# Expert stage: U rows gathered and dotted first, half of V's columns read densely and multiplied on TensorE

## The reference, cut to what matters

```python
q = (hblk @ w_q).reshape(b_, PEER_BLOCK, PEER_HEADS, 2, PEER_QDIM // 2)
s1 = einsum('bthd,hnd->bthn', q[..., 0, :], k1)   # 8 heads, 128 keys
s2 = einsum('bthd,hnd->bthn', q[..., 1, :], k2)
v1, i1 = top_k(s1, 16); v2, i2 = top_k(s2, 16)
cand = v1[..., :, None] + v2[..., None, :]        # 16 x 16 sums
score, pos = top_k(cand, 16)
idx = (i1 * 128 + i2 at pos)                      # one of 16384 experts
gate = softmax(score)
act = gelu(einsum('bthkd,btd->bthk', w_u[idx], hblk))
out = einsum('bthk,bthkd->btd', gate * act, w_v[idx])
```

## Time and profile before

| | |
|---|---|
| median of 3 runs | 2938.45 us (2937.06 to 2939.99) |
| profiled execution, span | 2939.0 us |
| PE busy | 2628.4 us (89%) |
| DVE busy | 1949.4 us (66%) |
| ACT busy | 979.2 us (33%) |
| POOL busy | 556.7 us (19%) |
| DMA | 901.77 MB, of that 604.02 MB by POOL's queue |
| granted PE clock | 0.988 of full speed |

### The profile page before, as it was taken

The page is one execution under the profiler, slowest core; times in us unless marked ns, Lnnn a source line. Parts: engine busy times, 40 slices in busy tenths (PEclk is TensorE's granted clock), DMA queues, the critical chain, the costliest instruction groups (busy, mean ns, idle before and its releaser), DMA issues.

```text
span 2939.0 us, 30782 instructions
## 1 busy us (share of the span) xinstructions
PE 2628.4 (89%) x11045; PEld 1777.7 (60%) x11045; DVE 1949.4 (66%) x2654; ACT 979.2 (33%) x1335; POOL 556.7 (19%) x580
## 2 busy tenths in 40 slices
PE   7999998999999999999999897777878877777777
PEld 3588886888777899998888753332434333232232
DVE  4679997444676788887555866666556656556646
ACT  5577776433564443334444211111101111111110
POOL 0000000000000000000000453433333333333333
PEclk9999999999999999999999999999999999999999
DMA  8733334542425888887566899999999999999998
GB/s 351 278 108 114 114 129 158 189 170 101 154 90 233 332 322 335 322 336 279 203 247 266 357 422 421 421 421 421 421 421 421 421 421 421 421 421 422 422 421 342
DMA packets 126356, 901.77 MB, mean 307 GB/s; under 512 B 14000, under 2 KB 15536, under 8 KB 17200
## 3 DMA queue, kind: packets, MB, share of 16 engines
q0 software_dynamic: 82944, 604.02, 49.8%
q1 hardware_dynamic: 38448, 276.84, 25.1%
q10 hardware_dynamic: 4864, 19.61, 1.7%
HBM read 898.29 MB, written 2.13 MB: 306 GB/s over the span
## 4 chain that ended last, share of the span: by engine, by line
PE 53%; DMA 35%; DVE 6%; issue 4%; ACT 1%; POOL 0%; POOLq 0%; SPq 0%; ACTq 0%; DVEq 0%
DMA u<-in_peer_u,idx 32%; PE ps L476 12%; PE ps L519 8%; PE ps L521 8%; PE ps L520 8%; PE ps L491 6%; DVE u L2042 3%; PE ps L882 2%; DMA v<-in_peer_v,idx 2%; PE ps L599 2%; PE ps L905 1%; DMA w<-in_stream 1%; PE ps L533 1%; PE ps L711 1%; PE ps L694 1%
## 5 line engine op out<-in xcount | busy, mean ns | idle before, releaser
L905 PE MATMUL ps<-v,dg 128*128 128x512 f32 x1920 | 894.4, 614 | 252.3 <-DMA v<-in_peer_v,idx 212.2
L2042 DVE SCALAR_TENSOR_TENSOR u<-u,hN 128x2048 f32<-128x2048 f32 x256 | 586.6, 2292 | 459.8 <-DMA u<-in_peer_u,idx 459.4
L905 PEld LDWEIGHTS ps<-v,dg 128*128 128x128 f32 x1920 | 356.4, 194 | 784.9 <-issue 427.9
L1383 DVE TENSOR_TENSOR wl<-w,wh 128x1024 fp32r<-128x1024 f32 x428 | 519.7, 1222 | 359.2 <-ACT wh L1018 358.8
L1018 ACT ACTIVATE wh<-w 128x1024 fp32r<-128x1024 f32 x428 | 451.3, 1059 | 607.9 <-PE ps L521 405.6
L2148 POOL DMA_INDIRECT u<-in_peer_u,idx x256 | 257.6, 1006 | 933.0 <-DVE u L2042 543.5
L476 PE MATMUL ps<-both,wh 128*128 128x256 f32 x2048 | 371.8, 284 | 0.0
L1326 ACT ACTIVATE dg<-con,wt 128x128 f32<-128x128 f32 x240 | 92.7, 399 | 807.4 <-PE ps L905 802.4
L476 PEld LDWEIGHTS ps<-both,wh 128*128 128x128 f32 x2048 | 320.1, 192 | 3.5 <-issue 3.3
L476 PE MATMUL ps<-both,wl 128*128 128x256 f32 x1024 | 289.8, 283 | 0.0
L2132 POOL DMA_DIRECT2D mr<-in_wmod x64 | 34.1, 534 | 1322.8 <-DVE br_lo L1791 912.7
(11 more groups left out here) (297 smaller groups left out, 2893.5 us busy)
## 6 DMA issues: line engine op xcount, KB each, us to landing
w<-in_stream SPq DMA_DIRECT2D x258, 1024.0 KB, 4.9
mr<-in_wmod POOLq DMA_DIRECT2D x64, 1024.0 KB, 6.9
wg<-in_gates ACTq DMA_DIRECT2D x8, 512.0 KB, 3.2
wx<-in_stream SPq DMA_DIRECT2D x4, 1024.0 KB, 7.9
u<-in_peer_u,idx POOLq DMA_INDIRECT x256
v<-in_peer_v,idx POOLq DMA_INDIRECT x256, 18.0
xs<-in_ctx ACTq DMA_DIRECT2D x1, 2048.0 KB, 7.6
xs<-in_x ACTq DMA_DIRECT2D x1, 2048.0 KB, 14.6
```

The lines of the kernel that those rows point to most:

```text
L905: last = mm(ps[:, b, :], dg[:, k % 4, :], V[n % NV][:, b * 512:(b + 1) * 512], start=(k == 0), stop=(k == TOPK - 1))
L1383: tt(wl[p % SPLITS][:, :, :], W[s][:, q * PIECE:(q + 1) * PIECE, :], wh[p % SPLITS][:, :, :].bitcast(F32), ALU.subtract)\
L2042: stt(U[n % NU][:, :], U[n % NU][:, :], 1.0, hN[t][:, :], ALU.mult, ALU.mult, accum_out=dot[:, t, k:k + 1])\
```

## The change

All 256 U rows are now gathered first, in the order `ORDER`: turn (0,0), turn (1,0), then heads 1 to 7 of tile 0, then heads 1 to 7 of tile 1. There are eight buffers `U`. All dots are on DVE (`ON_POOL` is empty); from the third turn on the tokens' tile is read from a copy in PSUM banks 0 to 3 that ACT makes (`spread_h`), except in turn 9.

When all rows of a tile are dotted, its 128 weights per token are worked out at once. V is then handled in two halves of 1024 columns:

- Columns 0 to 1023 are dense. For each token n a matrix of 128 x 128 weights over all experts is made: DVE writes two one-hot tiles over the token's 128 slots (`onehot`: `oa` for the first index, `ob` for the second index times the weight), PE multiplies them (`token`), and ACT copies four such matrices into `WT[t]` (`store_weights`). Tile 0's tokens are spread over the dots of tile 1 (`TOKEN_AT`, from row 149 to row 251); tile 1's come after all dots. Then PE runs over 128 blocks j of V, each a dense 0.52 MB load by SP into one of six buffers `VD`, four matmuls each (`dense`), into PSUM banks 0 to 3.
- Columns 1024 to 2047 are gathered, 256 half-rows of 4 KB per token into four buffers `VG`, and DVE adds each, times its weight, to `acc` (`gathered`).

Both halves of V are laid out as arrays of their own. The modulation row `m5r` is loaded by DMA instead of being spread by PE, and the last operations work on halves.

```diff
+DC = 1024
+ORDER = [(0, 0), (1, 0)] + [(0, h) for h in range(1, PH)] + [(1, h) for h in range(1, PH)]
+ON_POOL = ()
+ROUTE_AT = (1, 2, 4, 6, 7, 9, 11, 12, 14)
+TURN0 = 9
+TOKEN_AT = {n: TURN0 * TOPK + 5 + n * 103 // P for n in range(P)}
...
-        NU, NV = 4, 8
+        NU, NG, ND = 8, 4, 6
@@ @block.sync
+            for j in range(NKEYS):
+                if j == 0:
+                    sp.wait_ge(*AR.at(PH - 1, "q"))
+                elif j == 2:
+                    sp.wait_ge(*PR.at(2 * PH - 1, "s"))
+                elif j == 4:
+                    sp.wait_ge(*VG_.at(1, "g1"))
+                elif j >= ND:
+                    sp.wait_ge(dense_done, j - ND + 1)
+                sp.dma_start(VD[j % ND][:, :], a_vd[j]).then_inc(vd_in[j % ND], 16)
@@ @block.tensor
+            def token(t, n):
+                m = t * P + n
+                pe.wait_ge(onehots, m + 1)
+                if m % 4 == 0 and m >= 8:
+                    pe.wait_ge(w_stored, m // 4 - 1)
+                mm(ps[:, (4, 7)[m // 4 % 2], n % 4 * P:(n % 4 + 1) * P], oa[m % 6][:, :], ob[m % 6][:, :], start=(n % 4 == 0), stop=True,
+                   skip_group_check=True).then_inc(w_made, 1)
+            def dense(j):
+                pe.wait_ge(vd_in[j % ND], 16 * (j // ND + 1))
                 for t in (0, 1):
+                    for b in range(DB):
+                        last = mm(ps[:, DB * t + b, :], WT[t][:, j, :], VD[j % ND][:, b * 512:(b + 1) * 512], start=(j == 0), stop=(j == NKEYS - 1))
...
+            tables(1)
+            for n in range(P):
+                token(1, n)
+            pe.wait_ge(w_stored, 2 * P // 4)
+            for j in range(NKEYS):
+                dense(j)
@@ @block.scalar
+            def store_weights(g):
+                t, n = divmod(4 * g, P)
+                act.wait_ge(w_made, 4 * g + 4)
+                fn(WT[t][:, :, n:n + 4].rearrange("p i t -> p t i"), ps[:, (4, 7)[g % 2], :].rearrange("p (t i) -> p t i", t=4), ACT.Copy).then_inc(w_stored, 1)
@@ @block.vector
+            def onehot(t, n):
+                m = t * P + n
+                if m >= 6:
+                    dve.wait_ge(w_made, m - 5)
+                tsc(oa[m % 6][:, :], iota_k[:, :], i1T[:, n:n + 1], None, ALU.is_equal)
+                tsc(ob[m % 6][:, :], iota_k[:, :], i2T[:, n:n + 1], wT[:, n:n + 1], ALU.is_equal, ALU.mult).then_inc(onehots, 1)
+            def gathered(m):
+                t, c = m % 2, m // 2
+                dve.wait_ge(vg_in[m % NG], 16 * (m // NG + 1))
...
+                    dve.wait_ge(summed, m - 1)
+                    stt(acc[:, t, :], VG[m % NG][:, :], dot[:, t, c:c + 1], acc[:, t, :], ALU.mult, ALU.add).then_inc(summed, 1)
...
+            for r in range(ROWS):
+                q, k = divmod(r, TOPK)
+                t, h = ORDER[q]
...
+                    hv = hN[t][:, :] if q in (0, 1, TURN0) else ps[:, 0:4, :].rearrange("p b n -> p (b n)")
+                    dve.wait_ge(u_in[r % NU], 16 * (r // NU + 1))
+                    stt(U[r % NU][:, :], U[r % NU][:, :], 1.0, hv, ALU.mult, ALU.mult, accum_out=dot[:, t, h * TOPK + k:h * TOPK + k + 1])\
+                        .then_inc(dve_dots, 1)
+                if (q == 0 and k) or (q == 1 and k < 14) or (q > 1 and k in ROUTE_AT):
+                    next(routes, None)
...
+                for n in range(P):
+                    if TOKEN_AT[n] == r:
+                        onehot(0, n)
+            gelu_inner_of(1)
+            weights_of(1)
+            copy_tables(1)
+            for n in range(P):
+                onehot(1, n)
+                if n % 8 == 7:
+                    gathered(n // 8)
+            for m in range(P // 8, ROWS):
+                gathered(m)
@@ @block.gpsimd
+            for m in range(ROWS):
+                t, c = m % 2, m // 2
+                if m == 0:
+                    pool.wait_ge(*VR.at(2 * PH - 1, "idx"))
+                elif m == 1:
+                    pool.wait_ge(dve_dots, dots_by(ROWS - 1))
+                elif m == 3:
+                    pool.wait_ge(*VG_.at(1, "w"))
+                elif m >= NG:
+                    pool.wait_ge(summed, m - NG + 1)
```

More of the change, by code:

```diff
@@ L399, in build, with dots_by, pool_by, row_used @@
+        def dots_by(r):
+            return sum(1 for n in range(r + 1) if n not in ON_POOL)
+        def pool_by(r):
+            return sum(1 for n in ON_POOL if n <= r)
+        def row_used(r):
+            return (act_dots, pool_by(r)) if r in ON_POOL else (dve_dots, dots_by(r))
+        PRIMED_V = [VT, VL] + VO + [VS, VW]
+        PRIMED_A = [AD, AL] + AO + [AS]
+        PRIMED_P = [PL]
         block = ctx.enter_context(nc.Block())
@@ L896, in experts @@
[L896 to L920, removed]
+                pe.wait_ge(*VR.at(q - 2, "ib1"))
@@ L942, in _ @@
-            for h in range(PH):
-                if h == PH - 1:
-                    spread_m5()
-                experts(h, 0)
-                if 6 <= h + 4 < PH:
-                    route(h + 4)
-                if h + 1 < PH:
-                    experts(h, 1, h + 2 if h + 2 < PH else None)
-            last_half()
+            queries(1)
+            scores(2)
+            queries(2)
+            scores(3)
+            queries(3)
+            queries(4)
+            scores(4)
+            queries(5)
@@ new lines, in _ @@
+            queries(6)
+            scores(5)
+            queries(7)
+            for q in range(6, TURN0 + 4):
+                scores(q)
+            pe.wait_ge(*AR.at(PH - 1, "q"))
+            tables(0)
+            for q in range(TURN0, 2 * PH):
+                for n in range(P):
+                    if TOKEN_AT[n] // TOPK == q:
+                        token(0, n)
+                if q + 4 < 2 * PH:
+                    scores(q + 4)
+            tables(1)
+            for n in range(P):
+                token(1, n)
@@ new lines, in _ @@
+            assert next(routes, None) is None
+            gelu_inner_of(1)
+            weights_of(1)
+            copy_tables(1)
+            for n in range(P):
+                onehot(1, n)
[3 more added lines that the diff above has]
+                gathered(m)
+            dve.wait_ge(m5_in, 16)
+            dve.wait_ge(summed, ROWS)
+            for t in (0, 1):
+                tt(acc[:, t, :], acc[:, t, :], m5r[:, DC:D], ALU.mult).then_inc(*VX.inc(f"m{t}"))
+                dve.wait_ge(*VX.at(0, f"m{t}"))
+                tt(x2[:, t, DC:D], x2[:, t, DC:D], acc[:, t, :], ALU.add).then_inc(*VX.inc(f"o{t}"))
@@ L2132, in _, with product @@
                 pool.dma_start(mr[n % NM][:, :], a_wmod[n]).then_inc(mr_in[n % NM], 16)
[L2134 to L2136 removed]
+            def product(r):
+                t, _ = ORDER[r // TOPK]
+                pool.wait_ge(u_in[r % NU], 16 * (r // NU + 1))
+                nc.gpsimd.tensor_tensor(U[r % NU][:, :], U[r % NU][:, :], hN[t][:, :], ALU.mult).then_inc(pool_products, 1)
+            for r in range(ROWS):
+                q, k = divmod(r, TOPK)
+                if r == 0:
```

566 lines of the change are left out of this document (257 added, 309 removed).

## The result

The changed kernel takes 3056.45 us (median of 4 runs, 3046.63 to 3060.48) against 2938.48 us: a ratio of 1.0399, 95% interval 1.0381 to 1.0416. It is slower, as forecast, but by 118 us and not by 47. The profiled execution is the shortest of the four runs, with a span of 3044.8 us.

A forecast was written before the change was run, and what follows sets the result against it. DMA bytes were taken to bound the expert stage. From 1631.9 us, stage A was to end at 2417, B at 2505, C at 2971, and a 14 us tail gave 2985, 1.6% slower; range 2925 to 3055.

The forecast's parts named there:

- stage A: All 256 U dots, routing and tile 0's one-hots: bound by DVE at 780 us plus 5 for hiccups, ending at 2417.
- stage B: Weights and one-hots of tile 1 after all dots, DMA nearly idle: 88 us, ending at 2505.
- stage C: Dense product beside the gathered half of V, gathers ending last: 466 us, to 2971.
- tail: Last sum, last operations on halves and the store: 14 us, to 2985.
- PE in stage C: The dense product's matmuls, 3.43 us for each of 128 blocks: 439 us.
- The gathers in stage C: Half-rows of V at 2.0 us each beside the dense product, 219 in 439 us, then 17 at 1.6.
- The turn of a buffer: One gather buffer's gap, issue, landing, sum and 0.6 for POOL held up: 6.3 us for four buffers, 1.6 a gather.
- PE last: Rival for the stage's end: gathers keep up at 1.96 us, dense product runs without wait; end 2951, chance 0.16.
- Dearer one-hots or 4 KB descriptors: Rival: one-hot pairs at 0.64 us (+36) or descriptors at 393 GB/s (+30); end 3015 to 3050, chance 0.18.
- Nearly free one-hots: Rival in stage A and stage B: 0.30 us a pair, 51 us less; end 2900, half effect 2925; chance 0.16.
- POOL starved: Rival in stage C: every gather issue waits under a DVE sum, 2.4 us a gather; end 3085, chance 0.08.
- signs named for a wrong forecast: Stage A ending before 2380 or after 2450, trough under 60 us, PE dense waits over 20, POOL issues above 1.8.

The follow-up runs named there:

- the kernel with six blocks: The changed kernel with 122 of the 128 dense blocks of V left out, loads and matmuls; span 2968.9 us.

## Why the prediction was wrong

The direction, the three stages and the engine that ends last were right; the size of one term was not. Term by term, with the forecast against the profiled span, which is 10 us under the median span (against the median time the forecast is off by 71):

| step | forecast | measured | difference |
|---|---|---|---|
| first dot | 1631.9 | 1626.8 | -5 |
| stage A | 785 | 772 | -13 |
| stage B | 88 | 80 | -8 |
| stage C | 466 | 552 | +86 |
| tail | 14 | 13 | -1 |
| end | 2985 | 3044.8 | +60 |

- **Stage A.** Right, and DVE waited only 0.7 us for rows. From 1700 to 2399 us DMA's rate was 356 GB/s, 0.85 of the 421, as forecast; its share stayed at 0.93, not at 0.8. Dots from PSUM took 2278 ns. A pair of one-hots cost 0.455 us for 0.50, which is 6 of the 13 us. Not one unknown here was far off, because each was bounded by rows of like form.
- **Stage B.** Right; DMA fell to a share of 0.38 in it, the trough that was named.
- **PE in stage C.** 439 forecast, 439.7 measured.
- **The gathers in stage C.** This is the step that failed: "I take 2.0: in 439 us 219 gathers, 17 left at 1.6 = 27." Measured were 2.40 beside and 1.96 alone, so 183 and 57. The turn of a buffer was put at 6.3 us alone and is 7.8. The sum of 1.29 was right. The issue with its hold-up was put at 0.94 and 0.6 and took 1.25, so it was too dear by 0.3. The landing was not right: "about 3.2 to landing" came from a plain load of 0.5 MB, and a gather of the same bytes takes 5.5 from issue, 4.3 of it behind the issue, so 1.1 more (7.2 from issue beside the dense stream). And gaps and hand-overs took 1.0 for 0.30. And "1.96, and with queueing up to 2.15" was no upper bound at all: it started from the rate that DMA could leave over and added a little, when the turn beside the product is 4 x 2.40 = 9.6 us. The page of the kernel before had a row that warned, 1 MB from POOL's own queue, beside SP's stream:

```profile
mr<-in_wmod POOLq DMA_DIRECT2D x64, 1024.0 KB, 6.9
```

The kernels with three and six buffers show that the count of buffers was what mattered.
- **Rate of DMA.** I asked whether 4 KB descriptors would run at 393 or 421. With enough in flight they run at 409; in the changed kernel 371 was seen because too few were. The Trainium skill (DMA: Bandwidth & Descriptors, section Bandwidth) gives 6.15 us for a 1 MB transfer issued from GpSimd, the time of the issue left out. The row above agrees roughly: 6.9 us, 0.53 of it the issue.
- **Rivals.** PE last: no, it ended 112 us before the last sum, and in the kernel with six blocks the gathers alone take 474 us. Dearer one-hots or 4 KB descriptors: neither. Nearly free one-hots: no, 0.455. POOL starved: its number, 2.4 us a gather, is the one measured beside the product, by coincidence; its mechanism is not. With the same sums from SBUF and six buffers the pace was 2.06, although POOL was busier with each (146.87 us for 99 in the window above, against 98.51 for 84). And with the hold-up removed and four buffers the paces were 2.29 and 1.88: 240 sums at these would take 192 x 2.29 + 48 x 1.88 = 530 us instead of 552. So the hold-up is worth about 22 us of stage C, by one run, and the forecast had charged 0.6 us a turn for it where 0.3 were measured.
- **The range.** 2925 to 3055 missed the median by 1.5 us and held the profiled run. It was built with a top for stage C that no row supported. None of the signs named for a wrong forecast appeared (stage A ended at 2399, the trough lasted 80 us, PE did not wait for dense tiles, POOL's issues averaged 1.22 us): none of them looked at the ring.
- **A reading.** The issue held by a dot ended 0.8 us after it by the earlier trace rows, not 0.9; no term hangs on it.

What stays open: of the turn of 7.8 us about 4.3 lie between the end of the issue and the landing, and no run divides them further. Nor is it shown why the landing grows by 1.7 us beside the dense stream. The runs of the changed kernel also differ by 14 us among themselves, and only the shortest was profiled.

## What to carry to other kernels

A ring of buffers has a pace of its own: the time of a full turn (issue, landing, use, hand-over) over the number of buffers. Work it out before using the DMA's rate, and take the landing time from a transfer of the same kind; if the bytes of one turn of all buffers over its time are less than the full rate, the ring is the limit, whatever DMA share the profile shows. Splitting a stage that two resources shared into stages of one resource each costs what each leaves idle: here 159 us of bytes were saved, and the span grew by 106 even so, so 265 us were lost, until one-hots went to the idle engine and buffers were added.

## What the runs showed of the hardware

- Gathers of 0.524 MB in 4 KB rows with nothing beside them, by their pace: 221 GB/s with three buffers (0.524 MB in 2.37 us), 266 with four (a window of the kernel with six blocks), 374 with six (1.40 us). Beside the dense stream both together moved 371 with four and 409 with six or eight. Rows of 8 KB with twelve buffers ran at 421.
- The profile's DMA share was 0.98 at 371 GB/s and 1.03 at 409: a share near one does not say that the rate is at its top.
- POOL's product of two SBUF tiles holds up DVE as well as the other way round: 4.55 us for a 16-element operation. A dot with one PSUM operand is not held (2.28 us). Nor are only operations on two tiles held: a cast of 128x32 went from 163 to 1364 ns on average.
- ACT's copy of 128x512 from PSUM took 1055 ns when it wrote elements 512 B apart, against 592 for the plain form before. It was covered by DVE.
